# Attention in steps of two heads whose score products alternate in the row halves, conv taps dealt by units, selection passes over more steps

## The reference

```python
for each block of 128 queries (8 of them, tile t):
    logits = einsum(q_idx, k_idx) * 64 ** -0.5            # 8 index heads of 64
    score = einsum(w_idx, relu(logits))                   # one score for each key
    score = where(causal, score, -inf)
    sel = top_k(score, 256)                               # keys kept for this query
    s = einsum(q, k[sel]) * 64 ** -0.5                    # 8 heads of 64, 2 kv heads
    p = softmax(s); o = einsum(p, v[sel])
conv_out = silu(layernorm(depthwise_conv31(a * sigmoid(g)) + conv_b))   # 512 channels
x = x + gt1 * (concat(o, conv_out) @ w_out)
```

## Time and profile before

| | |
|---|---|
| time, median of 3 runs | 2960.3 us (2959.57 to 2964.39) |
| the profiled execution | 2961.0 us, span 2959.3 us |
| busy over the span | PE 2756.0, DVE 1650.5, ACT 793.5, POOL 1207.2 us |
| mean granted TensorE clock | 0.970 |
| index stage to the end of the attention | 140 to 779 us |

### The profile page before, as it was taken

One profiled execution on the slowest core, in us unless ns is written; L12 is line 12 of the kernel. 1 busy time (PEld: TensorE's weight loads), 2 busy tenths in 40 slices (PEclk: granted clock), 3 DMA queues, 4 the chain that ended last, 5 costly groups with the idle time before them and its releaser, 6 DMA issues.

```text
span 2959.3 us, 34689 instructions
## 1 busy us (share of the span) xinstructions
PE 2756.0 (93%) x13488; PEld 2276.7 (77%) x13488; DVE 1650.5 (56%) x2118; ACT 793.5 (27%) x1346; POOL 1207.2 (41%) x796
## 2 busy tenths in 40 slices
PE   4987978999999999999999999788889999999998
PEld 4866766788778888888886768677778888888887
DVE  6288866652566566566566684355535344444335
ACT  4236376443232111000113342222214000111002
POOL 2421356764454344344332323343344344344332
PEclk8999989999999999999999999899999999999999
DMA  6201011110321111111112110000031111111111
GB/s 212 65 12 33 15 50 50 58 58 20 124 71 50 43 57 45 40 57 50 46 50 93 43 36 29 0 1 1 29 128 58 50 57 43 43 57 50 38 55 57
DMA packets 142489, 153.34 MB, mean 52 GB/s; under 512 B 7183, under 2 KB 105252, under 8 KB 142374
## 3 DMA queue, kind: packets, MB, share of 16 engines
q1 hardware_dynamic: 136512, 141.87, 15.2%
q10 hardware_dynamic: 5862, 9.89, 0.9%
HBM read 143.35 MB, written 8.39 MB: 51 GB/s over the span
## 4 chain that ended last, share of the span: by engine, by line
PE 80%; DVE 11%; ACT 4%; issue 3%; POOL 1%; DMA 1%; ACTq 0%; SPq 0%; DVEq 0%; POOLq 0%
PE ps L1930 10%; PE ps L1931 10%; PE ps L1932 10%; PE ps L1915 10%; PE ps L1917 10%; PE ps L1916 10%; PE ps L2317 3%; PE ps L2089 2%; DVE yt L1752 2%; ACT sel_out L950 1%; PE ps L2115 1%; PE ps L2116 1%; PE ps L2117 1%; PE ps L2079 1%; DVE yt L1741 1%
## 5 line engine op out<-in xcount | busy, mean ns | idle before, releaser
L1915 PE MATMUL ps<-h_hi,w_hi 128*128 128x512 f32 x1472 | 585.6, 398 | 10.3 <-issue 5.6
L1917 PE MATMUL ps<-h_hi,w_lo 128*128 128x512 f32 x1472 | 575.4, 391 | 0.0
L1916 PE MATMUL ps<-h_lo,w_hi 128*128 128x512 f32 x1472 | 575.3, 391 | 0.0
L697 POOL TENSOR_TENSOR w_hi<-raw,zero 128x1024 fp32r<-128x1024 f32 x128 | 243.9, 1905 | 780.0 <-PE ps L1917 397.2
L1930 PE MATMUL ps<-w_hi,u_hi 128*128 128x512 f32 x1024 | 399.0, 390 | 0.0
L1931 PE MATMUL ps<-w_lo,u_hi 128*128 128x512 f32 x1024 | 398.8, 389 | 0.0
L1932 PE MATMUL ps<-w_hi,u_lo 128*128 128x512 f32 x1024 | 398.8, 389 | 0.0
L1081 ACT ACTIVATE act_r<-ps 128x512 f32<-128x512 f32 x128 | 76.5, 598 | 1130.7 <-PE ps L1917 1130.7
L1636 DVE TENSOR_TENSOR act_r<-act_r 128x512 f32<-128x512 f32 x128 | 167.5, 1309 | 328.9 <-ACT act_r L1081 328.8
L700 POOL TENSOR_TENSOR w_lo<-raw,w_hi 128x1024 fp32r<-128x1024 f32 x128 | 338.2, 2642 | 10.0
L1915 PEld LDWEIGHTS ps<-h_hi,w_hi 128*128 128x128 f32 x1472 | 278.1, 189 | 77.7 <-issue 17.8
(11 more groups left out here) (421 smaller groups left out, 4379.6 us busy)
## 6 DMA issues: line engine op xcount, KB each, us to landing
raw<-in_w_up_dram SPq DMA_DIRECT2D x64, 512.0 KB, 4.1
raw<-in_w_down_dram SPq DMA_DIRECT2D x64, 512.0 KB, 3.2
raw<-in_w_ada_dram SPq DMA_DIRECT2D x48, 512.0 KB, 3.8
raw<-in_w_in_dram SPq DMA_DIRECT2D x32, 512.0 KB, 3.7
raw<-in_w_out_dram SPq DMA_DIRECT2D x32, 512.0 KB, 3.2
x<-in_x_dram SPq DMA_DIRECT2D x8, 512.0 KB, 11.1
x<-in_x_dram ACTq DMA_DIRECT2D x8, 512.0 KB, 6.6
x_mid<-x SPq DMA_DIRECT2D x8, 512.0 KB, 5.4
```

The lines of the kernel that those rows point to most:

```text
L697: g_.tensor_tensor(w_hi[:, r, :], raw[:, r, :], zero.to_broadcast([P, 1024]), ALU.add).then_inc(sem("w_hi_done"), 1)
L1915: mm(ps[:, bank, :], wh, h_hi[:, k, cols], start=(k == 0), stop=False)
L1916: mm(ps[:, bank, :], wh, h_lo[:, k, cols], start=False, stop=False)
L1917: last = mm(ps[:, bank, :], wl, h_hi[:, k, cols], start=False, stop=(k == NK - 1))
```

## The change

- Attention goes by pairs of heads. `pair_mm` multiplies two heads of different row halves with alternating matmuls, one into banks 0 and 1, the other into 2 and 3. `index_pair` uses the same function, with the order of its matmuls unchanged. The order of heads is 0,5,1,4,2,7,3,6 in place of 0,4,1,5,2,6,3,7. The scores of a pair wait for both masks of the pair before. Transposes of a head come two steps behind its mask, and the values of both heads of a pair after its second head's transposes.
- The taps are dealt by units: 31 in six steps each for units 0 to 3, then in 10, 8, 10 and 10 steps, so that a unit ends with a step.
- Top-k: 8 rounds in the index stage (24 before); 32 beside the q projection (28 before); 12 and 12 after it, the last 12 of them of tile 3 (of tile 4 before); all 32 rounds of tile 4 in attention steps 0 to 23 (20 before).
- Bisection: 8 passes early (10 before), 24 passes in attention steps 0 to 34, two in three steps (22 in steps 0 to 21 before). The final parts of tiles 5, 6 and 7 move to steps 35 to 38, 41 to 46 and 48 to 53.

```diff
-        EARLY_ROUNDS = 24
+        EARLY_ROUNDS = 8
...
-        TOPK_Q, TOPK_K, TOPK_LAST = 52, 2 * ROUNDS, 12
+        TOPK_Q, TOPK_K, TOPK_LAST = 40, 52, 12
         TOPK_SLOTS = {4: range(0, 24)}
-        SEL_EARLY, SEL_ROUNDS = 10, 3
-        SEL_AT = {k - SEL_EARLY: k for k in range(SEL_EARLY, SEL_PASSES)}
+        SEL_EARLY, SEL_ROUNDS = 8, 4
+        SEL_AT = {n: SEL_EARLY + k for k, n in enumerate(n for n in range(36) if n % 3 < 2)}
         FIN_SLOTS = {}
-        for ti, at_slots in zip(SEL_TILES, ((23, 24, 25, 27, 28, 29), (32, 33, 35, 36, 38, 40), (43, 44, 45, 46, 47, 48))):
-            for part, n in enumerate(at_slots):
-                FIN_SLOTS[n] = ("sel_fin", ti, part)
-        HALF_TAPS, HALF_SLOTS, TAP_SLOTS = NCC * CONV_K, 25, 62
+        for ti, at_slots in zip(SEL_TILES, (range(35, 39), range(41, 47), range(48, 54))):
+            for part in range(6):
+                FIN_SLOTS.setdefault(at_slots[part * len(at_slots) // 6], []).append(("sel_fin", ti, part))
+        UNIT_SLOTS = (0, 6, 12, 18, 24, 34, 42, 52, 62)
...
-            if n <= HALF_SLOTS:
-                return min(5 * n, HALF_TAPS)
-            return HALF_TAPS + min(n - HALF_SLOTS, TAP_SLOTS - HALF_SLOTS) * HALF_TAPS // (TAP_SLOTS - HALF_SLOTS)
+            n = min(n, UNIT_SLOTS[-1])
+            u = max(m for m in range(2 * NCC) if UNIT_SLOTS[m] <= n)
+            n0, n1 = UNIT_SLOTS[u], UNIT_SLOTS[u + 1]
+            return CONV_K * u + -(-CONV_K * (n - n0) // (n1 - n0))
...
-            for i in range(NH):
-                n = NH * t + i
+            for i in range(0, NH, 2):
                 MICRO.append(("scores", t, i))
...
+                last = [(t, i - 2), (t, i - 1)] if i else [(t - 1, NH - 2), (t - 1, NH - 1)]
+                for e in range(2):
+                    n = NH * t + i + e
+                    if n >= 2:
+                        MICRO.append(("turn",) + last[e])
+                    MICRO.append(("mask", t, i + e))
+                    if n - 1 in SEL_AT:
+                        MICRO.append(("sel_step", SEL_AT[n - 1], 0))
+                    if taps_by(n + 1) > taps_by(n):
+                        MICRO.append(("conv", taps_by(n), taps_by(n + 1)))
...
+                    MICRO.append(("exp", t, i + e))
+                    MICRO += [(kind, half, 0) for kind, half in LN_SLOTS.get(n, [])]
+                    if e and n >= 2:
+                        MICRO += [("values",) + last[0], ("values",) + last[1]]
...
+                    MICRO += FIN_SLOTS.get(n, [])
+                    if n in SEL_AT:
+                        MICRO.append(("sel_pass", SEL_AT[n], 0))
...
-        HEADS = [j + 4 * half for j in range(4) for half in range(2)]
+        HEADS = [0, 5, 1, 4, 2, 7, 3, 6]
...
-            def score_mm(w, b, q, k, row, full):
...
+            def pair_mm(w, b, q, k, full):
+
+                kh, kl = k
                 for c0 in range(0, w, HALF):
                     cn = min(HALF, w - c0)
...
+                    for m, (l, r) in enumerate(((0, kh), (0, kl), (1, kh))):
+                        for e in range(2):
+                            row = slice(HD * e, HD * (e + 1))
+                            last = mm(ps[:, b[e] + c0 // HALF, 0:cn], q[e][l][row], r[row, c0:c0 + cn], start=(m == 0), stop=(m == 2))
+                last.then_inc(sem(full), 2)
...
-                    u = unit_of[kind, t, i]
-                    if u >= 2:
-                        pe.wait_ge(sem(units[u - 2][0]), units[u - 2][1])
+                    n = NH * t + i
+                    if n:
+                        pe.wait_ge(sem("masked"), n)
...
+                    first = HEADS[i] // 4
+                    j = [h % 4 for h in sorted(HEADS[i:i + 2])]
+                    pair_mm((t + 1) * P, (2 * first, 2 - 2 * first), [(q_hi[:, t % 2, c, :], q_lo[:, c, tok]) for c in j],
+                            (k_hi, k_lo), "score_full")
```

More of the change, by code:

```diff
@@ L458, in build @@
+                if t and i == 0:
                     MICRO.append(("divide", t - 1, 0))
-                if t and i == 1:
+                if t and i == 2:
                     MICRO.append(("out", t - 1, 0))
-        assert taps_by(TAP_SLOTS) == 2 * HALF_TAPS
-        MICRO += [("turn", NT - 1, NH - 1), ("ln_gate", 1, 0), ("values", NT - 1, NH - 1), ("divide", NT - 1, 0),
+        assert len(SEL_AT) == SEL_PASSES - SEL_EARLY
+        assert TOPK_K + TOPK_LAST == 2 * ROUNDS
+        assert taps_by(NT * NH) == 2 * NCC * CONV_K
@@ L463, in build @@
+        MICRO += [("turn", NT - 1, NH - 2), ("turn", NT - 1, NH - 1), ("ln_gate", 1, 0), ("values", NT - 1, NH - 2),
+                  ("values", NT - 1, NH - 1), ("divide", NT - 1, 0),
                   ("ln_silu", 1, 0)]
@@ L469, in build @@
         diag_end = [CONV_K * u + tap + n for u, tap, n in DIAGS]
-        unit_of, units = {}, []
-        for kind, t, i in MICRO:
-            if kind == "scores":
-                unit_of[kind, t, i] = len(units)
-                units.append(("masked", NH * t + i + 1))
         tp_of, tp_free = {}, []
@@ L1493, in _ @@
                 topk(t, r)
-                if n % SEL_ROUNDS == SEL_ROUNDS - 1 and n // SEL_ROUNDS < SEL_EARLY:
+                if n % SEL_ROUNDS == SEL_ROUNDS - 1:
                     sel_step(n // SEL_ROUNDS)
-            assert (TOPK_Q - EARLY_ROUNDS) // SEL_ROUNDS <= SEL_EARLY
-            for k in range((TOPK_Q - EARLY_ROUNDS) // SEL_ROUNDS, SEL_EARLY):
-                sel_step(k)
+            assert TOPK_Q - EARLY_ROUNDS == SEL_ROUNDS * SEL_EARLY
             dve.wait_ge(sem("tm_outq"), NT)
@@ L1518, in _ @@
                 cols = slice(t * HALF, (t + 1) * HALF)
-                if kind == "scores":
+                if kind == "mask":
                     bias = cmask[:, 2 * P - w:2 * P] if t < IDX_TILES[0] else score[t]
@@ L1522, in _ @@
                     n = NH * t + i
[L1523 to L1524 removed]
+                    dve.wait_ge(sem("score_full"), n + 1)
                     if n >= 2:
@@ L2017, in index_pair @@
                     pe.wait_ge(sem("relu_done"), n)
-                for c0 in range(0, w, HALF):
-                    cn = min(HALF, w - c0)
-                    for m, (q, k) in enumerate(((qh, ki_hi), (qh, ki_lo), (ql, ki_hi))):
-                        for e in range(2):
-                            row = slice(HD * e, HD * (e + 1))
-                            last = mm(ps[:, 4 + 2 * e + c0 // HALF, 0:cn], q[row], k[row, c0:c0 + cn], start=(m == 0), stop=(m == 2))
-                last.then_inc(sem("idx_full"), 2)
+                pair_mm(w, (4, 6), ((qh, ql), (qh, ql)), (ki_hi, ki_lo), "idx_full")
             def index_in(i):
```

55 lines of the change are left out of this document (13 added, 42 removed).

## The result

The changed kernel takes 2934.4 us (median of 4 runs, 2932.25 to 2937.48) against 2959.9 (2952.82 to 2964.39): ratio 0.992, 95% interval 0.990 to 0.994. It is 25.5 us faster; 61 were forecast, and the time lies above both ranges of the prediction (2885 to 2915, and 2873 to 2931 with the rivals). The profiled execution took 2937.5 us, span 2935.8. Each step is again placed by its mask on VectorE, so that a stretch of eight steps is one tile.

A forecast was written before the change was run, and what follows sets the result against it. It took TensorE as the bound from step 22 on and a ring of waits in steps 0 to 21; 2961.0 - 16 - 24 - 0 - 5 - 7 - 7 - 3 = 2899.0 us, range 2885 to 2915 (0.55).

The forecast's parts named there:

- Part 1: Top-k rounds and passes before the attention: index stage and k projection start sooner, -16 us, bounds -12 and -18.
- Part 2: Attention scores: a pair costs what one head costs now, saving 6.4 us at t=7, 5.6, 4.8, 4.0 at t=6 to 4.
- Part 3: Conv taps by units: 248 as before; the 9.4 us mid-step eviction wait goes, ScalarE waits up to 2.5 us instead.
- Part 4: Attention steps 0 to 31: 5.2 to 5.9 us a step, 180 us in all, -24 us, bounds +9 and -49.
- the ring: Steps 0 to 21: pass, part of the candidate step, then ScalarE's head work, 6.35 us a pass; 192 us if kept.
- Rival (d): Slower: pair scores wait for the second mask, 5 us at each of 32 pairs; 2960 to 2990 at worst; chance 0.05.
- the load sums: Steps 0 to 31: engines hold 149, 140, 133 and 129 us of work, so at least 149 to 155 us.
- Rival (a): Steps 0 to 31: the ring stays the pace and takes up the added rounds, gain 0 there; 2927; chance 0.15.
- (b): Better than forecast: steps 0 to 31 near 4.9 us each with full clock, -45 there; 2878; chance 0.15.
- (c): The halves don't overlap beside attention's other work, a pair costs two heads; 22 us lost in t=4 to 7; 2927; chance 0.05.
- Part 5: The tiles behind: t=4 0, t=5 -5, t=6 -7 and t=7 -7 us.
- Part 6: The tail: TensorE's 4.9 us idle time at otok falls to some 1.3 us, -3 us, bounds 0 and -6.

The follow-up runs named there:

- e9: Changed kernel with score and index pairs' products issued three of one head, then three of the other, not alternating; 2933.8 us (0.991).
- e16: Changed kernel with all products of one head (up to six) ahead of all of the other, in score and index pairs; 2956.2 us (0.999).
- e1: Changed kernel with the pairs of heads alone; rounds, passes, final parts and taps placed as in the kernel before; 2940.9 us (0.993).
- e3: Kernel before with only the taps dealt by units; 2951.0 us (0.998).
- e6: Changed kernel with pairs and taps by units only; rounds, passes and final parts placed as before; 2939.4 us (0.993).
- e8: Changed kernel with the top-k rounds of tile 4 left out, all but the last; 2913.6 us (0.984).
- e7: Changed kernel with the passes of steps 24 to 34 reading one column instead of whole rows; 2920.6 us (0.987).
- e10: Changed kernel with the final mask operations of tiles 5 to 7 on one column; 2926.6 us (0.989).
- e11: Changed kernel with GpSimd's additions of 1024 columns on one column; 2914.0 us (0.985).
- e5: Changed kernel with its 24 late passes one a step in steps 0 to 23, final parts nearly in the slots of before; 2931.7 us (0.990).
- e12: Changed kernel with taps ended at step 60 and the second half's layer norm two steps earlier; 2943.2 us (0.995).
- e4: Changed kernel with the transposes and masks of both heads of a pair ahead of all other work of the pair; 2941.3 us (0.994).
- e13: Changed kernel with each GpSimd addition of 1024 columns issued as four of 256, same sums; 2939.8 us (0.994).

## Why the prediction missed

The forecast was 2899 and the profiled execution took 2937.5 us, 38.5 more. By the prediction's own parts:

| part | forecast | measured | missed |
|---|---|---|---|
| 1, before the first mask | -16 | -15.6 | 0 |
| 4, steps 0 to 23 (161.1 to 132.8) | -28.3 | -15.7 | 13 |
| 4, steps 24 to 31 (43.2 to 47.2) | +4 | +11.6 | 8 |
| 5, t=4 | 0 | +8.1 | 8 |
| 5, t=5 and t=6 | -12 | -8.6 | 3 |
| 5 and 6, t=7 and the tail | -10 | -3.3 | 7 |

**Part 1 came out, partly by luck.** The first mask came at 339.4 (339 forecast), the k projection at 279.4 (277), the q projection at 233.8 (228.5). The index stage was mis-sized: TensorE left it 3.5 us sooner, not 8 (its last product ends at 228.9, before at 232.4), and the wait behind it was 4.85 us, not 4. What made it good was not forecast: TensorE's idle time ahead of k is 0.32 us where the sum left 3, and from k's start to the first mask it is 60.0 us against 62.2.

**Part 2 held for the tiles it named, and its reason was half right.** A pair of 1024 keys takes 1.60 us. Pairs alone saved 5.9, 5.6 and 7.1 us in t=5, t=6 and seven steps of t=7; 4.8, 5.6 and 5.6 (seven eighths of 6.4) were forecast. What the overlap needs is not alternation but nearness: e9 costs nothing, e16 costs 22 us. t=4 saved 3.4 of 4.0. In steps 0 to 31, where 10 us were to be saved, e1 shows 5.6, no more than the caution above allows: in most of them TensorE was not the bound. The Trainium skill (TensorEngine Tiling (Array Packing), PSUM Bottleneck) says that tiling leaves PSUM's evacuation as slow as it was, so that it may become the bound. The trace does not show that at t=7: TensorE is busy 41.4 of 43.2 us, VectorE 13.6. In steps 0 to 21 the masks do come late, though from VectorE's other work and not from reading PSUM.

**Part 3 held in kind.** The eviction wait is gone, and e3 alone gains 9 us; with the pairs it adds 2 to 3 (e6 against e1), within the noise. That the two share the slack that they make is likely, not shown.

**Part 4 failed, on two steps of its sum.** Its reading of the rows was off as well, at little cost: "Twenty-two passes, one a step, in 139.6 us" are 21 steps, as its own count of 21 passes says. The pace before was 6.58 us a pass (144.8 for 22), not 6.35, and the ring's 192 us would have been 197. The total of 204.3 us for steps 0 to 31 was right.

First, the length of a step: it put steps at 5.2, 5.5 and 5.9 us because "its candidate step is hidden" where there is no pass. It was not hidden. Candidate operations, stretched by GpSimd's additions, and the rounds stand ahead of the masks on VectorE. Leaving out the rounds gives 18.7 us in these steps, shortening the additions 14.6. The prediction saw one operation of 2.31 us beside an addition and used it as an argument against the lower bound, with no price; the additions cost 24 us before and 20 after. Twelve added rounds at 0.6 us are another 7, an estimate from e8's 18.7 us for 31. Rival (d), scores waiting for a late mask, does run, at 12.5 us of TensorE's waits in place of 60 to 90.

Second, steps 24 to 31: the load sums took ScalarE's 140 us over 32 steps as free to lie anywhere. But in tile 3 the first half's layer norm shares ScalarE, and copies that TensorE needs soon stand behind every pass in its queue. The passes there cost their own busy time, 13 us (e7), with TensorE's granted clock at 0.84 in that stretch and at 0.95 without them. Rival (a), no gain in steps 0 to 31, came nearest (4 us of gain), by this road and not by the ring that it named; (b) and (c) did not come up, since the halves overlap.

**Part 5, t=4 failed.** Six final parts in four steps, the last candidate step and the additions: final parts 2.8 us (e10), additions 6.8 (e11), together more than the 8.1 lost. Where the final parts are spread and the passes are over (e5), t=4 takes 43.1. The parts cannot be spread while the passes last until step 34, since the mask of tile 5 is due at step 40. t=6 missed 2.9 us; short final parts give 2.8 and short additions 2.6, each too small to be told from noise alone.

**Part 6 failed.** The idle time at otok went as forecast, to none; but it came back in another place, 5.84 us for the low part of the conv output. The prediction asked what otok waits for and not what is late next: otok and the products of the gate behind it start with the last values, which e12 shows by moving all else ahead. And t=7's 9.2 us are partly borrowed: behind the last mask stand 32 more matmuls before the 4.83 us wait that both kernels have some 115 us later (508 against 476 records), since values and transposes of two heads now lie behind it. From the last mask to the end of that wait it is 117.9 us against 112.5. In e1, e5, e6 and e16 the span behind the last mask is another 4 to 5 us longer. Up to 1000 us behind the mask, e5 and e6 are within 1 us of the changed kernel; the difference arises by 1150 us, in the second block, whose program is the same. What sets it off is not settled. In e4 it is 7 us, since its last mask stands 6 us earlier in the work.

What stays open: why steps 0 to 23 and t=4 trade some 4 us between kernels with the same program there, and how much of the gains of e7, e8 and e11 is the higher granted clock that comes with fewer waits (0.91 in steps 0 to 23 of the changed kernel, 0.97 in e8, 0.94 in e11).

## What to carry to other kernels

Work that runs in order on an engine costs by what stands behind it in the queue, not by the engine's load: before moving passes into other steps, list the copies that the bound engine needs there. Spreading the front of a chain over more steps also squeezes what has to follow before its due time. A stretched operation seen once in a trace should be multiplied by its count and priced before anything else; here what stretched it was worth 20 to 24 us, nearly as much as the whole change. And a stretch that is named by its steps should be checked against where those steps start.

## What the runs showed of the hardware

- Matmuls of the two row halves overlap without alternation when three of the other half stand ahead (1.60 us a pair), and only in part when six do (2.18 us).
- Operations of VectorE on 3 elements, 0.16 us undisturbed, average 0.49 to 0.67 us by line in steps 0 to 23 of the changed kernel, and 0.21 to 0.45 with GpSimd's additions beside them on one column; that edit saved 20 to 24 us. The Trainium skill (SBUF — State Buffer, Who interferes with whom) has a port pair that VectorE and GpSimd share, held by one at a time; the traces agree, and these runs show what it cost here.
- Four additions of 256 columns take 2.9 us against 2.39 for one of 1024, and did not let the small operations through well enough to pay (e13).
- Behind idle times of 1.9 and 5.8 us TensorE's rows show the half clock: eight values in 1.97 us at 520.42 (sixteen take 1.89 at full clock), a first product of 512 columns in 0.77 us at 760.39 (0.39 at full clock).
